# A two-layer hybrid decoder step in fp32: heads of a layer pipelined into each other, and every loop written out with constant waits

## What is computed

```python
h = rms_norm(x, norm1_g);  proj = h @ w_in            # u(512) | q(512) | k(512) | v(512)
q, k = rope(q), rope(k)                               # 4 heads, 2 components of 64 each
pool_y = (windowed mean of u  -  u) @ pool_w * pool_scale       # windows 2, 4, 8, 16; one per head
p = softmax(q k^T / 8) per component, causal;  a = p[0] - lam * p[1];  o = a @ v
x = x + concat(pool_y, rms_norm(o) * gain) @ w_out
a, b = split(rms_norm(x, norm2_g) @ w_up)             # d_ff = 2816
x = x + (silu(causal_conv3(a)) * b) @ w_down
```

## Time and profile before

| what | value |
|---|---|
| median of 3 runs | 3093.19 us |
| the profiled execution (its span, first to last instruction) | 3088.1 us |
| instructions in it | 45,465 |
| PE busy | 2837.5 us (92%) |
| DVE / ACT / POOL busy | 1545.4 / 785.2 / 932.2 us |
| mean granted TensorE clock | 0.936 |
| head stage, each layer (windows 61 to 735 and 1574 to 2243 us) | 674 and 669 us |
| inside the feed-forward part (795 to 1505, 2302 to 3022 us) | PE busy all the time, clock 1.00 |

### The profile page before, as it was taken

The page is one execution under the profiler, slowest core; times in us unless marked ns, Lnnn a source line. Parts: engine busy times, 40 slices in busy tenths (PEclk is TensorE's granted clock), DMA queues, the critical chain, the costliest instruction groups (busy, mean ns, idle before and its releaser), DMA issues.

```text
span 3088.1 us, 45465 instructions
## 1 busy us (share of the span) xinstructions
PE 2837.5 (92%) x16776; PEld 2587.2 (84%) x16776; DVE 1545.4 (50%) x1931; ACT 785.2 (25%) x1516; POOL 932.2 (30%) x768
## 2 busy tenths in 40 slices
PE   5889898988999999999988989888999999999996
PEld 4768686867999999999876867777789999999996
DVE  5746464555443444444575463647454444443435
ACT  3221313134222222222233131222332222222222
POOL 4624333244212212221254252525242121212220
PEclk7999898988999999999988998889889999999998
DMA  3422222121111111111113222321111111111111
GB/s 119 125 69 66 89 69 82 49 82 38 46 41 41 55 48 41 41 41 47 52 51 98 68 91 68 99 62 58 52 49 41 41 41 51 52 41 41 41 41 55
DMA packets 70800, 184.00 MB, mean 60 GB/s; under 512 B 8014, under 2 KB 28936, under 8 KB 70552
## 3 DMA queue, kind: packets, MB, share of 16 engines
q1 hardware_dynamic: 33352, 105.95, 10.1%
q0 software_dynamic: 18496, 67.58, 7.0%
q10 hardware_dynamic: 18848, 8.96, 1.0%
HBM read 169.27 MB, written 13.64 MB: 59 GB/s over the span
## 4 chain that ended last, share of the span: by engine, by line
PE 51%; issue 29%; POOL 10%; DVE 6%; ACT 2%; SPq 1%; POOLq 0%; ACTq 0%; DMA 0%; DVEq 0%
PE bank L921 22%; PE bank L950 9%; PE bank L1097 4%; POOL w_lo L498 4%; PE bank L1085 4%; PE bank L967 3%; PE bank L939 3%; PE bank L1132 3%; POOL act_lo L525 2%; PE bank L1112 1%; POOL page L562 1%; DVE rot L1412 1%; ACT scratch L764 1%; DVE scratch L1474 1%; POOL page L584 1%
## 5 line engine op out<-in xcount | busy, mean ns | idle before, releaser
L498 POOL TENSOR_TENSOR w_lo<-w_raw,w_hi 128x1024 fp32r<-128x1024 f32 x180 | 441.5, 2454 | 1474.2 <-ACT w_hi L630 1474.0
L1375 DVE TENSOR_TENSOR resid<-bank,resid 128x1032 f32<-128x1032 f32 x400 | 489.9, 1231 | 431.0 <-PE bank L950 431.0
L921 PE MATMUL bank<-act_hi,w_hi 128*128 128x344 f32 x2640 | 570.3, 324 | 0.0
L921 PE MATMUL bank<-act_hi,w_lo 128*128 128x344 f32 x2640 | 560.5, 320 | 0.0
L921 PE MATMUL bank<-act_lo,w_hi 128*128 128x344 f32 x2640 | 556.5, 319 | 0.0
L921 PEld LDWEIGHTS bank<-act_hi,w_hi 128*128 128x128 f32 x2640 | 439.6, 188 | 9.3 <-issue 0.4
L921 PEld LDWEIGHTS bank<-act_hi,w_lo 128*128 128x128 f32 x2640 | 446.3, 189 | 0.0
L921 PEld LDWEIGHTS bank<-act_lo,w_hi 128*128 128x128 f32 x2640 | 439.6, 188 | 0.0
L950 PE MATMUL bank<-mix_hi,w_hi 128*128 128x344 f32 x1200 | 291.5, 352 | 36.3 <-DVE resid L1375 36.3
L950 PE MATMUL bank<-mix_lo,w_hi 128*128 128x344 f32 x1200 | 259.3, 325 | 0.0
L950 PE MATMUL bank<-mix_hi,w_lo 128*128 128x344 f32 x1200 | 258.1, 324 | 0.0
(11 more groups left out here) (235 smaller groups left out, 3661.9 us busy)
## 6 DMA issues: line engine op xcount, KB each, us to landing
w_raw<-in_w_up SPq DMA_DIRECT2D x88, 512.0 KB, 3.5
w_raw<-in_w_down SPq DMA_DIRECT2D x44, 512.0 KB, 3.4
w_raw<-in_w_in SPq DMA_DIRECT2D x32, 512.0 KB, 3.4
w_raw<-in_w_out SPq DMA_DIRECT2D x16, 512.0 KB, 3.4
out<-v_tok ACTq DMA_DIRECT2D x16, 512.0 KB, 3.4
page<-in_x_prompt SPq DMA_DIRECT2D x4, 512.0 KB, 9.6
out<-page SPq DMA_DIRECT2D x4, 512.0 KB
out<-rows_out ACTq DMA_DIRECT2D x104, 4.0 KB
```

The lines of the kernel that those rows point to most:

```text
L498: pool.tensor_tensor(w_lo[:, slot, :], w_raw[:, slot, :], w_hi[:, slot, :].bitcast(F32), ALU.subtract).then_inc(w_lo_done, 1)
L921: ins = pe.matmul(g[:, t, 0:TW], w[:, slot, k * P:(k + 1) * P], x[:, k, t * TW:(t + 1) * TW], start=(k == 0 and n_ == 0), stop=(k == KC - ...
L1375: dve.tensor_tensor(tiles(resid[:, m, :]), grp3(u[0]), tiles(resid[:, m, :]), ALU.add).then_inc(g_free[u[0]], 1)
```

## The change

**Loops.** All `Fori` loops of all five engines, over layers, heads and feed-forward chunks, are written out. No wait value comes from a register any more.

**Heads.** Unit numbers, PSUM uses and semaphore counts come from tables (`unit_of`, `dense_uses`, `turns`, `extras`, `fills`):

```diff
-            with pe.Fori(0, DEPTH) as l:
+            for l in range(DEPTH):
...
+def extras(h):
+    early = [("v", h, t) for t in range(NT)] if h else [("u", 1, 0), ("u", 1, 1)]
+    at = {s: [] for s in range(QT_N)}
+    at[SOFT_STEP] = [("soft", h, 0), ("soft", h, 1)]
+    if h < N_HEADS - 1:
+        u = [("u", h + 1, t) for t in range(NT)]
+        at[0], at[1], at[3] = ([u[0]], [u[1]], [u[2]]) if h else ([], [u[2]], [])
+        at[5], at[6], at[7] = [("q", h + 1, 0)], [("q", h + 1, 1)], [("q", h + 1, 2)]
+    return early, at
...
+            def unit_tile(slot, t, out):
+                for k in range(KC):
+                    for n_, (w, x) in enumerate(PRODUCTS):
+                        ins = pe.matmul(out, w[:, slot, k * P:(k + 1) * P], x[:, k, t * TW:(t + 1) * TW],
+                                        start=(k == 0 and n_ == 0), stop=(k == KC - 1 and n_ == 2))
+                return ins
```

**Scores** have banks of their own (2, 3 and 4, 5, one pair for each component), component 1 first, and the turned weights take banks 2 and 3 again, all blocks in one go, with one copy on ACT:

```diff
-            for r, blocks in enumerate(rr):
-                to = (p_bank, t_bank)[r]
+            for b in range(i + 1):
+                ins = pe.transpose(p_pair[:, b * P:(b + 1) * P], probs[s % 2][:, 0, b * P:(b + 1) * P], ident)
+            ins.then_inc(p_full, 1)
+            if s + 1 < QT_N:
+                scores(s + 1, COMPS[0])
```

**Rotary embedding.** The four copies on DVE go; ACT issues four DMAs from SBUF to SBUF in their place, for q and for k:

```diff
+                def swap(dst, src, done):
+                    for a in range(4):
+                        to = 32 * (a ^ 1)
+                        act.dma_start(dst[to:to + 32, :], src[32 * a:32 * a + 32, :]).then_inc(done, 16)
...
+                    act.activation(tiles(kT[:, :]), grp3(u[0]), ACT.Copy).then_inc(g_free[u[0]], 1)
+                    released(act, u)
+                    swap(k_other, kT, k_swap)
+                    hi(6 * h + 3 if h else 5)
+                    for n, (at, width) in enumerate(qb_parts(h)):
```

**Second norm.** The split of the second feed-forward unit (b of chunk 0) moves from the last head to behind the norm:

```diff
-                norm(l * 2 + 1, l * T_LAYER + T0_NORM2)
+                norm(l * 2 + 1, t_head(l, ("norm", 1, 0)))
                 f0 = l * U_LAYER + U_FFN0
+                split_lo(f0 + 1, 1)
                 split_lo(f0 + 2, 2)
-                with pool.Fori(0, FC - 1) as i:
+                for i in range(FC - 1):
```

More of the change, by code:

```diff
@@ new lines, in extras, with fills @@
+def extras(h):
[7 more added lines that the diff above has]
+    return early, at
+def fills():
+    out, count = {}, [0, 0]
+    for l in range(DEPTH):
+        for h in range(N_HEADS):
+            early, at = extras(h)
+            turn = 0
+            for s in range(-1, QT_N):
+                for key in early if s < 0 else at[s]:
+                    b = turn if s < WEIGHTS_STEP - 1 else 0
+                    turn = 1 - b
+                    out[l, *key] = (b, count[b])
+                    count[b] += 1
+            out[l, "end", h] = tuple(count)
+    return out
@@ L546, in output_rms @@
                 pool.tensor_tensor(ss, ss, neghalf[0:rows], ALU.pow).then_inc(att_rms, 1)
-            with pool.Fori(0, DEPTH) as l:
+            for l in range(DEPTH):
                 n0 = l * U_LAYER
@@ L1099, in values @@
                         ins.then_inc(v_used, 1)
-                    def weigh(s):
+                    early, at_step = extras(h)
+                    pe.wait_ge(roped, it * 2 + 2)
+                    released(pe, use_head(l, ("out", h - 1, KC - 1) if h else ("v", 0)))
+                    fill(early[0])
+                    released(pe, use_head(l, ("y", h)))
+                    for c in COMPS:
+                        scores(0, c)
+                    for key in early[1:]:
+                        fill(key)
@@ L1153, in _ @@
+                        for b in range(i + 1):
+                            ins = pe.matmul(o_bank[:, 0:P], turned[:, b * P:(b + 1) * P], v_tok[:, b, :],
+                                            start=(b == 0), stop=(b == i))
+                        ins.then_inc(o_full, 1)
+                        for key in at_step[s]:
+                            fill(key)
                         if s == WEIGHTS_STEP:
+                            pe.wait_ge(f_free[1], FILLS[l, "end", h][1])
                             pe.wait_ge(soft_sel, it + 1)
@@ L1551, in _ @@
                 dve.memset(ext[:, 0:2], 0.0).then_inc(dve_step, 1)
-                dve.wait_ge(dve_step, fstep)
+                dve.wait_ge(dve_step, fstep + 1)
                 taps(0)
-                with dve.Fori(0, FC - 1) as i:
+                for i in range(FC - 1):
                     gate_b(i, use_ffn(l, i, 0))
```

1109 lines of the change are left out of this document (627 added, 482 removed).

## The result

| | before | after |
|---|---|---|
| median (4 runs each, side by side) | 3092.01 us | 3005.06 us |
| ratio, 95% interval | | 0.9721 (0.9707 to 0.9734) |
| span of the profiled execution | 3088.1 us | 3003.1 us |
| mean granted clock | 0.936 | 0.942 |
| instructions | 45,465 | 39,214 |

The forecast was 2938 us with a range of 2875 to 2995: the direction is right, the size is not, and the measured time lies 10 us above the range. The span fell by 85 us where the sum had 154.

The account below looks back on a forecast made before the run. PE's rate was taken as the bound, plus its waits and half-clock losses in the heads. 3088.1 - 154 (heads) + 4.6 (second norm) - 5 (feed-forward loops) = 2933 profiled, so 2938 us predicted, range 2875 to 2995.

Parts of the forecast that it names:

- Removed: 22.1 of waits and 10.2 of half clock, leaving 134.8: In each head of 167.1 us, PE's old waits and half-clock losses go, before the new order's costs are added.
- A middle head, 143.7: Heads 1 and 2 of each layer were to take 143.7 us, 23.4 less than before.
- The stall behind `qb`, 2.9: PE waits 2.9 us for ACT's copies to free its groups after `qb`; bounds 2 to 4.
- Step 0, 1.5: First attention step of a head: turning v's two halves, between exponentials on ACT, makes PE wait 1.5 us.
- Steps 1 and 3, 1.6 covered, 9.2 bare: Waits for combined weights in wide attention steps: 1.6 us with fill matmuls, 9.2 in head 3 without them.
- Head 0, 147.8: Each layer's first head: no earlier head's projection, but six fills of head 1; 147.8 us.
- Clock, 4.5 in a head and 6.0 at the end: Half-clock loss: 3.5 us at cache weights and slow scores plus 1.0 behind `qb`; 1.5 more for the last projection.
- The swap costs nothing: Four DMAs swapping q or k land in 3.5 us together, early enough in a middle head to add no wait.
- Rival 2: DVE and POOL become a second bound in the heads through clashes and the key chain: 70 us, giving 3005; chance 0.18.
- rival 4: Feed-forward loops: constants do not give the forecast's -5 us, so the time is 2943; no separate chance given.
- Rival 3: Written-out code starves PE of instructions: at 2.8 us a chunk +123 us, 3061; chance 0.04, of which 0.03 slower.
- Rival 1: Most new waits in the heads are covered: half of 58 us a layer, giving 2880; chance 0.20.

Follow-up runs that it names:

- fill_late: Kernel after, with the third tile of the next head's u moved from step 3 to step 4 in the four middle heads: 3048.63 us, ratio 0.9869.
- fillers: Kernel after, plus 24 matmuls nobody reads in each bare step (step 3 of head 0, steps 1 and 3 of head 3): 2998.74 us, ratio 0.9705.
- early turnings: Kernel after, with turnings of sampled rows and v ahead of the step loop, in heads 1 and 2 behind the next u's first tile: 2980.66 us, ratio 0.964.
- keys_short: Kernel after, but GpSimd multiplies only 128 of the 1024 columns of each cached key page: 3009.03 us, ratio 0.973.
- ffn_loop: Kernel after, with the feed-forward chunks put back into a loop on all five engines, heads still written out: 3003.47 us, ratio 0.9723.
- qb_first: Kernel after, with ScalarE copying qb out of PSUM ahead of the swap of k and the next unit's split: 3033.87 us, ratio 0.9815.
- balance: Kernel after, with qb copied first on ScalarE, four VectorE additions ahead of or between the rotation's operations, and key sums later: 3062.57 us, ratio 0.9906.

## Why the prediction was right and wrong

- **PE's rate is the bound, what can go is waits and clock.** Right: the work of a middle head stayed at 127 to 131 us through all orders, and what moved the time was the rest.
- **Removed: 22.1 of waits and 10.2 of half clock, leaving 134.8.** The waits are right within 5 us (83 in four heads, where 4 x 22.1 is 88). The clock was too small: 56 us in four heads, 14 each, by the windows. The work was 535 before and 520 after, where I left 533. So this part of the sum was 13 too long and hid some of the error below; why the new order's work fell by 15, where I had taken off 6, no run shows.
- **A middle head, 143.7.** 145.3 and 148.0 look right, but by luck: the waits are 10.4 where I had 6.0, the clock 5.4 and 8.3 where I had 4.5, and the work 3.8 less.
- **The stall behind `qb`, 2.9.** 3.0 to 3.3 in six heads. Right in cause and size (the rows give 0.39, not 0.50, from an issue to the next work; the 2.1 for four issues was 2.4 to 2.7). That it stands alone was wrong: four runs show the swap of k and DVE's list right behind it.
- **Step 0, 1.5.** 2.8 + 0.75 us. I had counted the turning of v, and not that the copy of the turned weights (1.02) and an exponential stand ahead of the sampled rows' copies on ACT. 2 us too little in each of eight heads.
- **Steps 1 and 3, 1.6 covered, 9.2 bare.** 1.4 and 8.8. Right.
- **Small hand-overs.** Some 2.4 us a head (mix_lo 0.9, a_T 1.2, kT 0.3) that the sum left out.
- **Head 0, 147.8.** 174.5. Of the 26.7 us, 12 are waits: k rotated late, 3.9 and 0.8 more on the turning behind it; the low parts of the first unit, 1.9, which the kernel before had too; step 0. 17 are clock, and the work was 2 less.
- **Clock, 4.5 in a head and 6.0 at the end.** This is the step that failed. 51 us in a layer where I put 20. In the middle heads 5.4 and 8.3 came, but I left the term the same for heads whose steps are bare, though I had priced those very waits at 4 to 5 us. `fill_late` shows what belongs to them: 7 us of clock for 3 of wait. The covered runs place part of the 31 us: over the eight heads, each up to the next one's first row or the first feed-forward unit's, (1 - clock) x busy is 108 us in the change, 86 with the bare steps covered (`fillers`), 88 with the early turnings and 70 with both. That is 11 us a layer for the bare steps and 10 for step 0; the rest is not placed.
- **Waits, 38 in a layer.** 61, the smaller miss: 12 us more in head 0, 4.4 in each middle head and 2.2 in head 3, the latter from step 0 and the small hand-overs.
- **The sum of a layer** is therefore 591 + 23 (waits) + 31 (clock) - 13 (work) = 632, as measured.
- **The swap costs nothing.** One DMA took 2.4 us to landing for q and 5.0 for k. I took 3.5 for all four, but in heads 1 to 3 the last of k's is there 8.3 to 9.6 us after the first issue, 23 us into head 1 where I had 18.5. In the change itself no wait of PE ends on it; true as forecast, and only so long as other stalls stay.
- **Clashes: I counted none.** Rival 2 put them on the key chain. They came in head 0, on k's rotation, and cost 9 us in one layer and 5 in the other, as `keys_short` shows. Its full 70 us did not come. That the time it named, 3005, is the measured one is chance (its own sum gives 2938 + 70 = 3008). The Trainium skill, "SBUF — State Buffer", the part on the two sides of the memory, says that the one of the two engines that comes second is blocked until the other's instruction is done. The rows agree where POOL has one instruction (2.3 us); where it has five in a row, the 12.39 us show VectorE blocked through all of them.
- **Second norm, +4.6.** 2.2 us in each layer: right.
- **Loops, -5.** Nothing (`ffn_loop`): rival 4. The longer starts of parts with a register operation ahead were not what set the chunk's length.
- **Rival 3, starved PE.** Nothing: units are 35.43 us apart with 2.18 MB of instructions, and 35.35 with 1.05 MB in `ffn_loop`. The rule in the Trainium skill, "Runtime: NRT & Kernel Launch", on instruction fetch, gave it no weight, and the trace agrees.
- **Rival 1, half the waits.** The opposite: 61 us of waits where I had 38.

## What to carry to other kernels

Write the time of a stage as work, plus waits, plus (1 - clock) x busy time, and forecast the last term for each place where a wait stays bare, not once for the stage: in `fill_late` 3 us more of bare wait cost 7 us of clock. The term is an estimate: the same order lost 1.6 us in one layer and 9.6 in the other. Work put into a bare step, even work that nobody reads, can pay a little (6 us here). Before removing a stall, list what else becomes ready at its end: where several queues are about equally long, a single repair may only change which of them is waited for.

## What the runs showed of the hardware

- VectorE can be held by GpSimd for a whole row of instructions: 12.39 us for an operation on 8 columns (0.23 alone), 5.30 us for one on a single column, 2.3 for one GpSimd instruction.
- Of four DMAs of 129 KB from SBUF to SBUF each took 2.4 us to landing when issued at a head's end. Those of k took 4.0 to 7.8 in heads 1 to 3, while pages and weights were loading, and 2.2 to 2.4 in head 0, where no page load was issued beside them. The four issues took ScalarE 2.4 to 3.1 us in the change, and up to 3.8 in `qb_first`.
- The granted clock of head 1 was between 0.87 (`balance`) and 0.99 (`early_turns`) with the same work in another order, and 0.93 and 0.99 in the two layers of one kernel (the early turnings with the unread matmuls). The heads 0 to 2 of the change agreed within 2.1 us from one profile to the next.
